# The sliding-window attention of the second block: streamed products ahead of the transposes, gating and sink differences on GpSimd

## The reference, cut to what matters

```python
h = rmsnorm_2(x, norm_g[l])
proj = h @ w_in[l]
q, k, v, za, u, vs, zs, gm = jnp.split(proj, IN_SPLITS, axis=-1)
...
s = jnp.einsum('bnqhgd,bnkhd->bhgnqk', qc, kb, ...) * (HEAD_DIM ** -0.5)
...
m = jnp.maximum(jnp.max(s, axis=-1, keepdims=True), sink)
p = jnp.exp(s - m)
denom = jnp.sum(p, axis=-1, keepdims=True) + jnp.exp(sink - m)
o = jnp.einsum('bhgnqk,bnkhd->bnqhgd', p / denom, vb.astype(jnp.float32))
...
a = (a * jax.nn.silu(za)) @ w_att_out[l]
sgo = (sgo * jax.nn.silu(zs)) @ w_sg_out[l]
```

## Time and profile before

| | |
|---|---|
| three runs, median (lowest to highest) | 1279.54 us (1279.12 to 1280.45) |
| the profiled execution | 1279.79 us |
| its span, first to last instruction | 1278.0 us |
| PE busy | 1261.3 us (99%) |
| DVE, ACT, POOL busy | 729.8, 548.2, 84.2 us |
| the attention stage, 859.2 to 959.4 us | 100.2 us |

### The profile page before, as it was taken

How to read it: one execution, slowest core, us unless ns; L and a number is a source line. 1 busy time by engine, 2 the same in 40 slices (tenths; PEclk the granted TensorE clock), 3 DMA queues, 4 the chain that set the end, 5 groups by cost and what they waited for, 6 DMA issues and landing times.

```text
span 1278.0 us, 15814 instructions
## 1 busy us (share of the span) xinstructions
PE 1261.3 (99%) x6114; PEld 1058.4 (83%) x6114; DVE 729.8 (57%) x1185; ACT 548.2 (43%) x953; POOL 84.2 (7%) x129
## 2 busy tenths in 40 slices
PE   9999999999999999999999999999999999999997
PEld 8878888888888888888888888878888888888886
DVE  6885677753635444444443349858985436436554
ACT  5456565642334434343322233338763343223233
POOL 0002250220000000000000000002220000000000
PEclk9999999999999999999999999999999999999999
DMA  6241323133532232333323323331104322323221
GB/s 199 68 116 53 83 75 91 51 85 96 181 99 77 89 107 90 99 98 115 99 83 100 115 66 116 99 99 34 50 19 157 118 84 87 102 96 99 84 98 66
DMA packets 106956, 119.54 MB, mean 94 GB/s; under 512 B 13895, under 2 KB 89741, under 8 KB 106893
## 3 DMA queue, kind: packets, MB, share of 16 engines
q1 hardware_dynamic: 106876, 118.67, 29.5%
q10 hardware_dynamic: 16, 0.00, 0.0%
HBM read 113.42 MB, written 2.10 MB: 90 GB/s over the span
## 4 chain that ended last, share of the span: by engine, by line
PE 90%; DVE 6%; ACT 3%; issue 1%; POOL 0%; ACTq 0%; DVEq 0%; POOLq 0%
PE ps_mm L2013 56%; PE ps_mm L2048 23%; PE ps_s L2191 1%; DVE w_lo L1216 1%; PE ps_o L2222 1%; PE ps_o L2440 1%; ACT w_hi L685 1%; PE ps_mm L2105 1%; PE ps_s L2244 1%; PE ps_t L2202 1%; PE ps_t L2427 1%; DVE w_lo L1225 1%; DVE small L1816 1%; PE ps_o L2271 1%; DVE pt_lo L1836 1%
## 5 line engine op out<-in xcount | busy, mean ns | idle before, releaser
L2013 PE MATMUL ps_mm<-act_hi,w_hi 128*128 128x512 f32 x944 | 372.4, 394 | 2.8 <-DVE w_lo L1216 2.8
L2013 PE MATMUL ps_mm<-act_hi,w_lo 128*128 128x512 f32 x944 | 369.9, 392 | 0.0
L2013 PE MATMUL ps_mm<-act_lo,w_hi 128*128 128x512 f32 x944 | 369.8, 392 | 0.0
L1216 DVE TENSOR_TENSOR w_lo<-stage,w_hi 128x2048 fp32r<-128x2048 f32 (+5 forms) x78 | 158.4, 2031 | 160.7 <-ACT w_hi L685 160.5
L2013 PEld LDWEIGHTS ps_mm<-act_hi,w_hi 128*128 128x128 f32 x944 | 177.4, 188 | 39.2 <-DVE w_lo L1216 4.5
L2013 PEld LDWEIGHTS ps_mm<-act_hi,w_lo 128*128 128x128 f32 x944 | 177.4, 188 | 35.5
L2013 PEld LDWEIGHTS ps_mm<-act_lo,w_hi 128*128 128x128 f32 x944 | 177.5, 188 | 34.7
L685 ACT ACTIVATE w_hi<-stage 128x2048 fp32r<-128x2048 f32 (+5 forms) x79 | 133.7, 1693 | 159.9 <-PE ps_mm L2048 112.7
L1622 DVE TENSOR_TENSOR w_lo<-stage,w_hi 128x2048 fp32r<-128x2048 f32 x23 | 52.7, 2292 | 56.3 <-ACT w_hi L965 56.2
L2048 PE MATMUL ps_mm<-w_hi,act_hi 128*128 128x512 f32 (+2 forms) x208 | 77.6, 373 | 0.6 <-DVE lat L1352 0.5
L2048 PE MATMUL ps_mm<-w_lo,act_hi 128*128 128x512 f32 (+2 forms) x208 | 77.1, 370 | 0.0
(11 more groups left out here) (401 smaller groups left out, 2031.9 us busy)
## 6 DMA issues: line engine op xcount, KB each, us to landing
stage<-in_w_in SPq DMA_DIRECT2D x43, 1024.0 KB, 5.3
stage<-in_w_ffn_gate SPq DMA_DIRECT2D x11, 1024.0 KB, 5.3
stage<-in_w_ffn_up SPq DMA_DIRECT2D x11, 1024.0 KB, 5.3
stage<-in_w_ffn_down SPq DMA_DIRECT2D x10, 1024.0 KB, 5.0
stage<-in_w_out SPq DMA_DIRECT2D x4, 1024.0 KB, 5.7
stage<-in_w_att_out SPq DMA_DIRECT2D x4, 1024.0 KB, 5.2
stage<-in_w_sg_out SPq DMA_DIRECT2D x4, 1024.0 KB, 5.5
stage<-in_w_o SPq DMA_DIRECT2D x4, 1024.0 KB, 5.1
```

Of the source, the lines that this page charges most:

```text
L1216: V.tensor_tensor(w_lo[:, s, 0:k * w], stage[:, s, 0:k * w], w_hi[:, s, 0:k * w].bitcast(F32), ALU.subtract).then_inc(w_lo_made, 1)
L2013: ins = T.matmul(ps_mm[:, 2 * bank_slot + m, :], wt[:, kk, m * P:(m + 1) * P], acts[ap][:, kk, :], start=(r == 0), stop=(r == per - 1), sk ...
```

## The change

Five things are changed, all between the za units and the end of the attention loop.

1. PE: within a step the streamed products stand ahead of the transposes of piece p - 3.
2. ACT: the upper part of the transposes stands behind the exponentials of piece p and the sink's exponential, no longer ahead of them.
3. DVE: the lower part of piece p - 4 stands at the top of step p; before, that of piece p - 3 stood near the end of step p. The gating stands behind the maxima.
4. POOL: takes the sink difference of piece p from DVE, and (tanh + 1) * z, now in two instructions (add 1, multiply). Its order in a step is sink difference of p, scaling of p - 1, then (tanh + 1) * z.
5. za units: ACT makes `w_hi` of unit u + 2 ahead of the Silu of unit u; DVE frees the banks first, makes `w_lo` of unit u + 2, and the lower parts of keys and values only then (the values' one round later).

```diff
+            pool.wait_ge(sink_landed, 16)
+            for p in range(WIN_STEPS + 2):
+                if p < WIN_PIECES:
...
+                    pool.wait_ge(win_max_made, p + 1)
+                    G.tensor_tensor(dsink[:, c:c + 2], sinkb[:, h:h + 3:2], nm2[:, j:j + 3:2], ALU.add
+                                    ).then_inc(sink_diff, 1)
+                if 1 <= p <= WIN_PIECES:
...
+                    pool.wait_ge(rden_made, q + 1)
+                    G.tensor_scalar(prob2[:, q % 4, 256 + j0:512], prob2[:, q % 4, 256 + j0:512], rden2[:, c + 1:c + 2],
+                                    None, ALU.mult).then_inc(win_p_ready, 1)
+                for u, m in WIN_STREAM.banks.get(p - 1, ()):
+                    n = 2 * (u - U0["zs"]) + m
+                    pool.wait_ge(z_tanh, n + 1)
+                    linked_after(G.tensor_scalar(tmp[:, m, :], tmp[:, m, :], 1.0, None, ALU.add))
+                    G.tensor_tensor(gu[:, n, :], tmp[:, m, :], gu[:, n, :], ALU.mult).then_inc(z_gated, 1)
...
-                if i:
-                    hi(u + 1)
+                if i < 3:
+                    hi(u + 2)
...
-                if LAG <= p < NP + LAG:
-                    q = p - LAG
-                    act.wait_ge(win_t_full, q + 1)
...
                     act.wait_ge(sink_diff, p + 1)
                     nc.scalar.activation(esink[:, c:c + 2], dsink[:, c:c + 2], ACT.Exp).then_inc(sink_exp, 1)
+                if LAG <= p < NP + LAG:
+                    q = p - LAG
+                    act.wait_ge(win_t_full, q + 1)
...
+                if LAG < p <= NP + LAG:
+                    q = p - LAG - 1
+                    dve.wait_ge(win_pt_hi_made, q + 1)
...
-                    dve.wait_ge(win_max_made, p + 1)
-                    V.tensor_tensor(dsink[:, c:c + 2], sinkb[:, h:h + 3:2], nm2[:, j:j + 3:2], ALU.add
-                                    ).then_inc(sink_diff, 1)
...
-                for u, m in WIN_STREAM.banks.get(p - 1, ()):
-                    z_bank(m, 2 * (u - U0["zs"]) + m)
...
+                stream(WIN_STREAM, p, lambda u: acts_x)
                 q = p - LAG
                 if 0 <= q < NP:
...
-                stream(WIN_STREAM, p, lambda u: acts_x)
```

More of the change, by code:

```diff
@@ L1750, in _, with turned_values @@
             normed(kv[:, 0, :], u, 1)
[L1752 to L1756, removed]
+            def turned_values():
+                return ps_t[:, :].rearrange("p (t g n) -> p t g n", t=TT, g=AG)
+            halves = (slice(0, AD), slice(AD, 2 * AD))
             for i in range(4):
                 u = U0["za"] + i
-                if i:
-                    lo(u + 1)
-                else:
+                if i == 0:
                     dve.wait_ge(v_turned, 1)
[L1765 to L1771, removed]
+                    for half in halves:
+                        V.tensor_copy(v2_hi[:, :, :, half], turned_values()).then_inc(v2_wg_made, 1)
+                for m in range(2):
+                    normed(gz[:, 2 * i + m, :], u, m)
+                if i < 3:
+                    lo(u + 2)
+                if i == 0:
                     for g in range(AG):
@@ L1777, in _ @@
                                             ).then_inc(k_lo_made, 1)
+                if i == 1:
+                    for n, half in enumerate(halves):
+                        dve.wait_ge(v2_wg_made, n + 1)
+                        V.tensor_tensor(v2_lo[:, :, :, half], turned_values(), v2_hi[:, :, :, half].bitcast(F32),
+                                        ALU.subtract).then_inc(v2_wg_made, 1)
                 V.scalar_tensor_tensor(out=res[:, i, :], in0=res[:, i, :], scalar=rstd[:, i:i + 1], in1=gf_b[:, :],
                                        op0=ALU.mult, op1=ALU.mult).then_inc(x3_made, 1)
-                for m in range(2):
-                    normed(gz[:, 2 * i + m, :], u, m)
                 if i == 3:
@@ L1796, in _ @@
             for p in range(WIN_STEPS + 2):
+                if LAG < p <= NP + LAG:
+                    q = p - LAG - 1
+                    dve.wait_ge(win_pt_hi_made, q + 1)
+                    keys = lambda x: x.rearrange("p (e n) -> p e n", e=2)[:, :, (0 if q // 8 else P):2 * P]
+                    V.tensor_tensor(keys(pt2_lo[:, q % 2, :]), keys(ps_t[:, :]), keys(pt2_hi[:, q % 2, :].bitcast(F32)),
+                                    ALU.subtract).then_inc(win_pt_lo_made, 1)
+                if p < NP:
+                    b, i = p // 8, p % 8
+                    h = window_head(i, 0)
+                    j = 16 * (b % 2) + h
+                    j0 = 0 if b else P
+                    dve.wait_ge(win_s_full, p + 1)
+                    mx = nmax[:, 2 * (p % 4):2 * (p % 4) + 2]
+                    after(link(V.tensor_reduce(mx, ps_s[:, p % 2, :].rearrange("p (e n) -> p e n", e=2)[:, :, j0:256],
+                                               AX.X, ALU.max, negate=True)))
+                    V.tensor_tensor(nm2[:, j:j + 3:2], mx, nsinkb[:, h:h + 3:2], ALU.min).then_inc(win_max_made, 1)
                 if p > LAG + 1 and (p - LAG - 1) % 2 == 0 and p - LAG - 1 <= NP:
```

42 lines of the change are left out of this document (12 added, 30 removed).

## The result

The changed kernel takes **1291.8 us** (median of four runs, 1291.5 to 1292.3) where the kernel before, on the same chip, takes 1279.65. The ratio is 1.0096, with a 95% interval of 1.0083 to 1.0108. The forecast was 1285.3: slower as said, but by 12.2 us and not by 5.8, and outside the range by 1.8 us. The profiled execution took 1292.07 us, with a span of 1290.3.

A forecast was written before the change was run, and what follows sets the result against it. PE, busy 99%, was taken as the bound, with a 2.98 us attention step. Terms -1.9 - 3.2 + 3.9 + 1.7 + 5.3 = +5.8 us gave 1285.3 us; range 1277.0 to 1290.0.

The forecast's parts named there:

- The za term: At the za units, PE's wait for the lower part of unit za + 2's weights goes: -1.9 us.
- A smaller step: At the za units, 2.5 us of DVE idle time cover the keys' and residual's instructions that move behind.
- The ring: In the attention, DVE and ACT wait for each other once per step: 3.15 us against PE's 2.98, 23 steps, +3.9 us.
- +0.57: DVE's half unit of weights exceeds its room by 0.57 us in even steps 12, 22 and 30: +1.7 us.
- the slack wins: Rival: DVE and ACT's turn in the attention stays under 2.98 us, both gains come in full, 1274.4 us; chance 0.12.
- The pair on POOL: (tanh + 1) * z as two POOL instructions delays sink differences (1.1 each) and minima (1.0 each) in the attention: +5.3 us.
- my slope of 1.57: POOL's scaling times for 128 and 256 columns, extended to 512, give 1.57 us for the addition; 1.3 was taken.
- the 2.6 us less by that page: By the page's 769 ns for POOL's addition, the two instructions are 0.5 us shorter, the sum some 2.6 us less.
- The old waits: In the attention, PE's existing waits at the transposes and their loads all go: -3.2 us, bounds 2.0 and 3.2.
- PE waits for `pt_lo` at the transposes in nearly every step: Sign in the attention from piece 8 on: PE waits there by 0.1 to 0.3 us per step.
- the forecast stage of 107.9 us: The attention stage was to take 100.2 - 3.2 + 10.9, about 107.9 us.
- the lock bites both ways: Rival: in six attention meetings POOL's instructions also wait behind DVE's two-input ones, about 6 us more, 1291 us; chance 0.08.

The follow-up runs named there:

- the kernel with both edits: The changed kernel with DVE's gating back at the top of its step and ACT's `pt_hi` ahead of the exponentials again: 1279.79 us.

## Why the forecast was right and wrong

**The za term** (-1.9) was right: 2.0 us. A smaller step failed behind it, that the instructions moved behind are covered by 2.5 us of idle time. That cover is in the first rounds. In the last round the residual stands behind the last banks, ahead of the maxima: +1.2, a term that I did not have. I looked where PE waited, and not at each round in which the order was changed.

**The ring** was right in mechanism and size: 3.15 us forecast, 3.14 to 3.16 measured where nothing else disturbs, in the kernel with the gating on top. It sets the pace in 20 steps (12 to 31) and not in 23: steps 8 to 11 take 2.67 to 2.89 us in the kernel with the gating on top and the pair on DVE. So the term of 3.9 us was about 0.5 too large. With a weights' half and a gating in it 3.69 and 3.70, so +0.54 instead of +0.57. The rival "the slack wins" fell with it.

**The pair on POOL** was right in both places (ACT waits 0.77 and 0.78 us in the late even steps, 1.39 and 1.14 in steps 6 and 10; the minimum takes 1.14 us in odd ones) and nearly in price (1.1 and 1.0 forecast; 1.0 each measured from step 15 on, 0.7 for step 10 with the gating on top). Two sizes were off. The addition takes 1.50 us, not 1.3, nearer to my slope of 1.57. And step 6, which I gave to the slack, costs 1.45 in the changed kernel and 0.9 with the gating on top: the half-wide pieces have the shorter PE step too, and the 1.2 us of slack were not there to spend.

The meeting of minimum and product agrees with the lock that the SBUF — State Buffer page of the Trainium skill, section "Who interferes with whom", describes between a DVE instruction with two SBUF inputs and a GpSimd instruction that reads SBUF. The scaling on POOL, which I had taken to be free of it by the earlier trace rows, is held up where DVE is first (changed kernel, timeline, DVE and POOL):

```profile
893.14 1.20 DVE L1240 TENSOR_TENSOR w_lo<-stage,w_hi 128x1024 fp32r<-128x1024 f32 x1
...
893.32 1.81 POOL L675 TENSOR_SCALAR prob<-prob,small 128x256 f32<-128x256 f32 x1 [1.00 <-DVE small L1846]
```

It takes 1.81 or 1.82 us instead of 0.93 in all six steps with a weights' half from step 12 on. In the earlier trace rows the scaling was first by 0.40 us, and DVE lost nothing; in the kernel with both edits DVE's subtraction begins 0.16 us into one scaling (888.36) and takes 1.39. What the longer scaling costs was not tested; in the kernel with the gating on top the step from 889.15 to 892.30 has such a scaling in it and takes 3.15 us, as the ordinary ones do.

The GPSIMD Engine Reference page of the Trainium skill, section "3.1 Elementwise — side-by-side cycle accounting", gives 769 ns for a tight loop over 512 elements; the measured 1.50 us decides, and the 2.6 us less by that page did not come.

**The old waits** (-3.2) went in name only. The waits at the transposes went; what PE's order took from them it gave to the products with the values, 3.4 us in the kernel before with PE's order alone. So the term of -3.2 was a gain that did not come.

**The missing term** is the main step that failed: the gating's place, put at nothing, where it costs 3.5 us. The change list has it ("the gating stands behind the maxima"), and my working put its 0.9 us into DVE's room beside the ring, where it fits. It did not ask who waits for it. PE does: the products of piece p - 4 overwrite `ps_o`, and the gating reads it. Behind `pt_lo` and the maxima it comes up to 1.5 us after PE, and since PE issues in order, the next scores are late as well and feed the ring. "PE waits for `pt_lo` at the transposes in nearly every step" failed for this reason as a sign, and is true of the kernel with the gating on top.

The sum, from the forecast stage of 107.9 us to 114.7: 4.2 for the gating (110.6 us is the stage with it on top; the clock's drop lies in these 4.2), 1.3 for the third scores, and 1.3 left. In the kernel with the gating on top the 21 steps from 11 to 31 take 72.3 us, 9.7 more than 21 times 2.98, where the forecast had 10.9 for 23. The starts of the scores, compared piece by piece with the kernel before, show where the rest lies: 1.3 us are lost at the third scores, 1.0 won back by piece 8, 9.0 lost from there to piece 31, and 1.2 behind the last scores, where PE waits 0.96 and 0.62 us for `pt_lo`. That is 10.5 where the forecast had 7.7 (10.9 less the old waits' 3.2). Beside the third scores it is the last steps, for which I had no term, that make up the difference; the middle fits to 0.3 us, but partly by luck, since the ring's term was too large and the first two pairs' was too small.

The rival "the lock bites both ways" came nearest in time, 1291, but by luck: in the meetings that it priced, POOL's addition took 1.50 us and its product 1.27 to 1.30 all eight times. Where DVE does hold POOL up, at the scaling beside the weights' halves, that rival had no price.

## What to carry to other kernels

When instructions on an engine are put in another order, write down for every one of them, also for those that are merely displaced, who waits for its result or for the buffer that it frees, and in every round of the loop, the last one above all. Two engines that hand work to each other twice in a step form a ring; add up its turn and compare it with the bound engine's step, since above it a further delay on its path is paid in full (5.7 us for a pair that costs 1.0 in an open ring). A move of independent work ahead of one wait takes it away from another: look at what it covered.

## What the runs showed of the hardware

An addition of a constant on GpSimd, one input of 512 columns, takes 1.50 us, longer than its two-input product of the same width (1.27 to 1.30); DVE does both in one instruction of 0.67.

A DVE minimum of two columns that begins 0.15 us into GpSimd's product takes 1.14 us instead of 0.16, so that for its size it pays the most. GpSimd's scaling of 256 columns that begins 0.18 us into DVE's subtraction of 1024 takes 1.81 us instead of 0.93; the other way round, DVE's subtraction takes 1.39 when it begins 0.16 us into the scaling and 1.22, as alone, when it begins 0.40 us into it.

Two waits of PE of 0.76 and 0.95 us were followed by 3.4 us at the lower clock in the profiled execution of the changed kernel. With the gating on top 8.2 us of waits in 11 places left the mean clock at 0.999.
